# A fifth pair of column blocks by seven products, with the convolution two blocks earlier and three sums of h on GpSimd beside it

## The reference, cut to what matters

```
h = rms_norm(x)
proj = h @ w_in        # r_q r_k r_v r_g | m_q m_k m_v m_o | m_i m_f | gate_r gate_m
ret = retention(rotary(r_q), rotary(r_k), r_v)       # 4 heads, 4 chunks of 128 tokens, a state from chunk to chunk
ret = head_norm(ret) * silu(r_g);       y_ret = ret @ w_ret_branch
qk = silu(conv4(m_q, m_k) + b)          # 4 taps along the tokens
hm = mlstm(q, k, m_v, m_i, m_f) * sigmoid(m_o)       # 4 heads, 4 chunks, a state from chunk to chunk
y_m = head_norm(hm) @ w_mlstm_branch
x += (sigmoid(gate_r) * y_ret + sigmoid(gate_m) * y_m) @ w_out
x += mixture of 32 experts (two per token);  rms_norm
```

## Time and profile before

| | |
|---|---|
| three runs, us | 1027.02, 1027.93, 1027.90 |
| profiled execution, us | 1028.9 |
| its span, first to last instruction, us | 1027.0 |
| busy PE / DVE / ACT / POOL, share of the span | 98% / 48% / 31% / 11% |
| transfers, MB and mean GB/s | 268.21 and 261 |
| chain that ended last, largest parts | PE 78%, SP's queue 12%, DVE 4% |

### The profile page before, as it was taken

One profiled execution on the slowest core, in us unless ns is written; L12 is line 12 of the kernel. 1 busy time (PEld: TensorE's weight loads), 2 busy tenths in 40 slices (PEclk: granted clock), 3 DMA queues, 4 the chain that ended last, 5 costly groups with the idle time before them and its releaser, 6 DMA issues.

```text
span 1027.0 us, 13106 instructions
## 1 busy us (share of the span) xinstructions
PE 1002.9 (98%) x4941; PEld 650.3 (63%) x4941; DVE 494.0 (48%) x796; ACT 316.9 (31%) x524; POOL 108.9 (11%) x119
## 2 busy tenths in 40 slices
PE   8999999999999999999999999999999999999895
PEld 7888888899988988888885433333333333333333
DVE  6267556567778768645525123233233333332235
ACT  6343564455555656622213000000000000000012
POOL 0688300030000000000000000000000000000000
PEclk9999999999999999999998999999999999999998
DMA  9223221422433525162989799999999999999993
GB/s 329 83 83 126 80 82 42 155 37 81 118 103 105 184 42 182 64 210 85 409 318 358 312 419 421 419 420 420 420 420 421 420 421 420 420 420 422 420 413 142
DMA packets 62579, 268.21 MB, mean 261 GB/s; under 512 B 9456, under 2 KB 9648, under 8 KB 37816
## 3 DMA queue, kind: packets, MB, share of 16 engines
q1 hardware_dynamic: 57464, 257.32, 63.1%
q0 software_dynamic: 4800, 9.98, 4.2%
q10 hardware_dynamic: 256, 0.10, 0.0%
HBM read 267.36 MB, written 4.20 MB: 264 GB/s over the span
## 4 chain that ended last, share of the span: by engine, by line
PE 78%; SPq 12%; DVE 4%; DMA 3%; issue 1%; ACT 1%; DVEq 0%; ACTq 0%
PE pj L648 30%; PE pj L923 14%; PE pj L825 13%; SPq L549 8%; PE pj L949 7%; SPq L546 4%; PE cb L605 3%; DMA raw_moe<-in_w_up_dram 3%; PE cb L959 2%; PE cb L960 2%; DVE sg L1934 1%; PE pj L891 1%; PE cb L668 1%; DVE raw_mix L1617 1%; PE cb L697 1%
## 5 line engine op out<-in xcount | busy, mean ns | idle before, releaser
L923 PE MATMUL pj<-raw_moe,xT 128*64 128x512 f32 x1016 | 227.6, 595 | 4.6 <-DMA raw_moe<-in_w_up_dram 2.5
L1458 DVE TENSOR_TENSOR wl<-raw_mix,wh 128x1024 fp32r<-128x1024 f32 x112 | 145.5, 1301 | 144.7 <-ACT wh L1103 144.4
L1918 DVE TENSOR_TENSOR x<-x,cb 128x512 f32<-128x512 f32 x120 | 77.0, 683 | 190.6 <-PE cb L960 190.6
L923 PEld LDWEIGHTS pj<-raw_moe,xT 128*64 128x64 f32 x1016 | 72.1, 137 | 141.2 <-issue 141.2
L1103 ACT ACTIVATE wh<-raw_mix 128x1024 fp32r<-128x1024 f32 x112 | 118.3, 1059 | 113.4 <-PE pj L648 75.8
L949 PE MATMUL pj<-raw_moe,hf 128*64 128x512 f32 x512 | 116.7, 598 | 1.7 <-ACT hf L1404 1.7
L949 PEld LDWEIGHTS pj<-raw_moe,hf 128*64 128x64 f32 x512 | 35.1, 136 | 66.9 <-issue 66.6
L648 PE MATMUL pj<-wh,hTh 128*128 128x512 f32 x192 | 76.5, 398 | 0.7 <-DVE hTl L1489 0.7
L648 PE MATMUL pj<-wl,hTh 128*128 128x512 f32 x192 | 74.9, 390 | 0.0
L648 PE MATMUL pj<-wh,hTl 128*128 128x512 f32 x192 | 74.8, 390 | 0.0
L1409 ACT ACTIVATE yh<-pj,now 128x512 fp32r<-128x512 f32 x32 | 20.5, 684 | 157.8 <-PE cb L960 143.6
(11 more groups left out here) (387 smaller groups left out, 1757.3 us busy)
## 6 DMA issues: line engine op xcount, KB each, us to landing
raw_moe<-in_w_gate_dram SPq DMA_DIRECT2D x64, 1024.0 KB, 26.5
raw_moe<-in_w_down_dram SPq DMA_DIRECT2D x64, 1024.0 KB, 26.6
raw_moe<-in_w_up_dram SPq DMA_DIRECT2D x63, 1024.0 KB, 26.5
raw_mix<-in_w_in_dram SPq DMA_DIRECT2D x32, 1024.0 KB, 5.6
raw_mix<-in_w_in_dram POOLq DMA_DIRECT2D x8, 512.0 KB, 5.8
raw_mix<-in_w_ret_branch_dram SPq DMA_DIRECT2D x4, 1024.0 KB, 6.5
raw_mix<-in_w_mlstm_branch_dram SPq DMA_DIRECT2D x4, 1024.0 KB, 5.5
raw_mix<-in_w_out_dram SPq DMA_DIRECT2D x4, 1024.0 KB, 5.1
```

Of the source, the lines that this page charges most:

```text
L923: mm = nc.tensor.matmul(pj[a * CAP:(a + 1) * CAP, up, :], xT[:, 4 * half + k, a * CAP:(a + 1) * CAP], weights_of(m + a)[:, k, :], start=ha ...
L1458: V.tensor_tensor(wl[:, q % RING, :, :], entry_source(q), wh[:, q % RING, :, :].bitcast(F32), ALU.subtract).then_inc(wl_ok, 1)
L1918: V.tensor_tensor(part, part, cb[:, 2 + g % 2, :], ALU.add).then_inc(c_add, 1)
```

## The change

- `FAST` gets the pair m_v as its first entry, so that m_v's two plain blocks become seven products; the plain blocks are now six, in the order r_q, r_k, m_q, m_k, r_v (two), and what stood beside blocks 2 and 3 stays beside blocks 2 and 3.
- The convolution moves to blocks 3 and 4. For m_q ScalarE applies Silu in one go, and VectorE's product falls away; for m_k all stays. `convx` gets a second buffer, so the copies of the second block don't wait for the first's convolution.
- The retention runs by pairs of heads: steps 0 to 7 (heads 0 and 1) two to a step of block 5, steps 8 to 15 (heads 2 and 3) one to a half x = 0 to 8 and their outputs up to x = 9.
- The mLSTM moves to x = 17 to 40, its decays to x = 9 to 13, the products of its queries to x = 12, 13, 15 and 20.
- GpSimd waits for the turned q and then forms `first21`, `second` and `fourth`, each term in four pieces of 256 columns; `third` follows when the convolution is over.
- The places of some tiles and the waits of the first quadrants change with it.

```diff
-B_RQ, B_RK, B_RV, B_MQ, B_MK, B_MV, B_RG, B_GR, B_GM, B_MO, B_WR, B_WM, B_WO = 0, 1, 2, 4, 5, 6, 8, 10, 12, 14, 16, 18, 20
+B_RQ, B_RK, B_MQ, B_MK, B_RV, B_MV, B_RG, B_GR, B_GM, B_MO, B_WR, B_WM, B_WO = 0, 1, 2, 3, 4, 6, 8, 10, 12, 14, 16, 18, 20
-FAST = (B_GR, B_RG, B_GM, B_MO)
+FAST = (B_MV, B_GR, B_RG, B_GM, B_MO)
+F0 = B_MV
-GATINGS = (5, 6, 11, 12, 14, 15, 18, 24)
-ATTENTION = [1 + (26 * i + 7) // 15 for i in range(16)]
+GATINGS = (5, 6, 11, 12, 15, 19, 20, 24)
+ATTENTION = [17 + (23 * i + 7) // 15 for i in range(16)]
+ML_FIRST = ATTENTION[0]
+DECAYS = (9, 10, 11, 12)
+DECAY_EXPS = (10, 11, 12, 13)
+QUERIES = (12, 13, 15, 20)
...
-        convx = at("convx", 80, [P, 4, 3 + T])
+        convx = [at(f"convx{s}", k, [P, 4, 3 + T]) for s, k in enumerate((80, 128))]
...
+        def ret_step(n):
+            return n % 8 // 2, 2 * (n // 8) + n % 2
...
                 if p == 0:
-                    sp.wait_ge(r_o, 12)
...
+                    sp.wait_ge(wl_ok, 4 * F0 - 4)
+                    quadrant(p, U_11, 0, 0)
+                    sp.wait_ge(wl_ok, 4 * F0 - 2)
+                    quadrant(p, U_T3, 0, 1)
+                    sp.wait_ge(conv_v, 4)
+                    quadrant(p, U_22, 1, 1)
+                    sp.wait_ge(wl_ok, 4 * F0)
+                    quadrant(p, U_21, 1, 0)
+                    return
+                if p == 1:
+                    sp.wait_ge(r_o, 14)
...
                         x = 2 * (PRODUCTS * p + u) + s
                         product_half(p, u, s)
-                        if x == 0:
+                        if x <= 8:
+                            ret_products(7 + x)
+                        if x <= 7:
+                            ret_scores(8 + x)
+                        if x == ML_FIRST - 1:
                             ml_scores(0)
...
+            def decay_exps(j):
+                if j == 0:
+                    act.wait_ge(gex_in, 1)
+                    nc.scalar.activation(gex[:, :, :], gex[:, :, :], ACT.Exp).then_inc(gex_ok, 1)
+                act.wait_ge(dt_in, j + 1)
+                nc.scalar.activation(dT[:, j, :], dT[:, j, :], ACT.Exp, scale=-1.0).then_inc(dt_ok, 1)
+                for c in range(TT):
+                    m = nc.scalar.activation(gbc[:, j, c * P:(c + 1) * P], gbc[:, j, c * P:(c + 1) * P], ACT.Exp, scale=-1.0,
+                                             bias=gcol[:, 3, 4 * j + c:4 * j + c + 1])
+                m.then_inc(wint_ok, 1)
...
                     if b in (B_MQ + 1, B_MK + 1):
                         n = 4 * (b - B_MQ - 1) + j
                         dst = (mqT, mkT)[n // 4]
                         act.wait_ge(free[j], b)
...
-                        nc.scalar.activation(dst[:, j, :], convx[:, j, 3:3 + T], ACT.Identity, scale=vcol[:, 56 + n:57 + n], bias=vcol[:, 24 + n:25 + n]).then_inc(conv_a, 1)
+                        nc.scalar.activation(dst[:, j, :], convx[n // 4][:, j, 3:3 + T], ACT.Identity, scale=vcol[:, 56 + n:57 + n], bias=vcol[:, 24 + n:25 + n]).then_inc(conv_a, 1)
                         act.wait_ge(conv_v, n + 1)
-                        if n >= 1:
+                        if n < 4:
+                            nc.scalar.activation(dst[:, j, :], dst[:, j, :], ACT.Silu).then_inc(mqk_ok, 1)
+                        else:
                             act.wait_ge(mqk_ok, n)
-                        nc.scalar.activation(csg[:, :], dst[:, j, :], ACT.Sigmoid).then_inc(conv_s, 1)
+                            nc.scalar.activation(csg[:, :], dst[:, j, :], ACT.Sigmoid).then_inc(conv_s, 1)
+                    if b == B_MK:
+                        act.wait_ge(rkT_ps, j + 1)
+                        nc.scalar.activation(rkT[:, :, j * P:(j + 1) * P], cb[:, j, :].rearrange("p (h l) -> p h l", h=H), ACT.Copy).then_inc(rkT_ok, 1)
...
             def combined(dst, first, terms):
                 for n, (term, op) in enumerate(terms):
-                    m = G.tensor_tensor(dst[:, :, :], (dst if n else first)[:, :, :], term.bitcast(F32), op)
+                    for k in range(4):
+                        m = G.tensor_tensor(dst[:, k, :], (dst if n else first)[:, k, :], term[:, k, :].bitcast(F32), op)
...
+            pool.wait_ge(rqT_ok, TT)
             combined(first21f, hTh[:, low, upper].bitcast(F32),
                      ((hTh[:, high, upper], ALU.subtract), (hTl[:, low, upper], ALU.add), (hTl[:, high, upper], ALU.subtract)))
             pool.wait_ge(rope_ok, 2 * TT + 1)
             combined(secondf, first21f, ((hTh[:, low, lower], ALU.subtract), (hTl[:, low, lower], ALU.subtract)))
-            pool.wait_ge(rqT_ok, TT)
+            pool.wait_ge(rope_ok, 2 * TT + 2)
+            combined(fourthf, secondf, ((hTh[:, high, lower], ALU.add), (hTl[:, high, lower], ALU.add)))
+            pool.wait_ge(mqk_ok, 8)
+            pool.memset(mva[:, :, :, DV:DA], 1.0)
             combined(thirdf, hTh[:, low, lower].bitcast(F32),
                      ((hTh[:, low, upper], ALU.subtract), (hTl[:, low, lower], ALU.add), (hTl[:, low, upper], ALU.subtract)))
-            pool.wait_ge(rope_ok, 2 * TT + 2)
-            pool.wait_ge(r_s, 16)
-            combined(fourthf, secondf, ((hTh[:, high, lower], ALU.add), (hTl[:, high, lower], ALU.add)))
```

More of the change, by code:

```diff
@@ L510, in _ @@
             sp.dma_start(bif[:, 1:2], b_f.rearrange("l h -> h l")).then_inc(wg_in, 16)
-            for n in range(MIX_RAW, 2 * B_RG):
+            for n in range(MIX_RAW, 2 * F0):
                 mix_chunk(n)
@@ L830, in product_half @@
                         m.then_inc(pair_used, 1)
-            for b in range(1, B_RG):
+            for b in range(1, F0):
                 block_of(b)
@@ L1323, in fast_half @@
                 after = ATTENTION.index(x - 1) if x - 1 in ATTENTION else -1
-                i = 0 if x == 1 else after + 1
-                if (x == 1 or after >= 0) and i < 12:
+                if x <= 9:
+                    ret_output(6 + x)
+                i = 0 if x == ML_FIRST else after + 1
+                if (x == ML_FIRST or after >= 0) and i < 12:
                     act.wait_ge(m_s, i + 1)
@@ L1350, in _ @@
             turned = {2 * (PRODUCTS * w[0] + w[1]) + w[2]: n[0] for w, n in TURNS.items() if len(w) == 3}
-            for b in range(B_RG):
+            for b in range(F0):
                 evict_block(b - 1)
                 block_of(b)
-            evict_block(B_RG - 1)
-            ret_output(15)
+            evict_block(F0 - 1)
             for p in range(len(FAST)):
@@ L1745, in block_of, with decays, queries @@
                         ml_normed(1 - (b - B_WR), b - B_WR)
-                if b == B_RV:
+                if b == B_MQ:
                     rq_turned(3)
+            def decays(j):
+                if j == 0:
+                    dve.wait_ge(gb_in, 16)
+                for c in range(TT):
+                    m = V.scalar_tensor_tensor(dT[:, j, c * P:(c + 1) * P], gbc[:, j, c * P:(c + 1) * P], gcol[:, 0, 4 * c + j:4 * c + j + 1],
+                                               kc[:, K_NOTYET:K_NOTYET + P], ALU.subtract, ALU.add)
+                m.then_inc(dt_in, 1)
+            def queries(j):
+                if j == 0:
+                    dve.wait_ge(mqk_ok, 8)
+                dve.wait_ge(wint_ok, j + 1)
+                V.tensor_tensor(gbc[:, j, :], gbc[:, j, :], mqT[:, j, :], ALU.mult).then_inc(wq_ok, 1)
             def upper_left(p, s):
-                dve.wait_ge(free[s], B_RG + 4 * p + U_11 + 1)
+                dve.wait_ge(free[s], F0 + 4 * p + U_11 + 1)
                 dve.wait_ge(full[2 + s], full_fast(p, U_21, s))
@@ L1756, in upper_right @@
             def upper_right(p, s):
[L1758 removed]
+                dve.wait_ge(free[s], F0 + 4 * p + 2)
                 h = home(p, 0, 1, s)
@@ L1824, in _ @@
             dve.wait_ge(c_in, 48)
-            for b in range(B_RG):
+            for b in range(F0):
                 block_of(b)
-            dve.wait_ge(r_out, 16)
-            dve.wait_ge(gex_ok, 1)
             for p in range(len(FAST)):
```

278 lines of the change are left out of this document (136 added, 142 removed).

## The result

| | before | after |
| --- | --- | --- |
| median of 19 runs each, us | 1027.22 (1025.79 to 1028.3) | 1029.4 (1028.41 to 1032.27) |
| profiled execution, its span, us | 1028.9, 1027.0 | 1029.35, 1027.5 |
| first matmul behind the fast pairs (block `B_WR`), us | 402.44 | 405.94 |
| first matmul of the logits, us | 542.41 | 545.90 |
| first expert's first matmul, us | 566.63 | 567.66 |

The changed kernel is slower by a ratio of 1.0021 (interval 1.0014 to 1.0028), +2.2 us; forecast was 1030.6, and 1029.4 lies within the forecast's own range. The mixer ends 3.5 us later, of which 1.0 us is left at the first expert in the profiled executions (that of the kernel before is one of its longer ones, 1028.9 against a median of 1027.22). So two things need reasons: the +3.5, and where a part of it went.

The account below looks back on a forecast made before the run. Up to 538 us TensorE's columns bound the kernel, then the experts' weight stream. -5.4 + 5.5 + 1.6 + 0.4 + 0.6 = +2.7 us gives 1030.6 us by the median; own range 1028.4 to 1032.5, range of the chances 1023.4 to 1033.2.

Parts of the forecast that it names:

- Products, -5.4: m_v's two plain blocks become seven products, 168 matmuls instead of 192 on TensorE: -5.4 us.
- Stall, +5.5: TensorE waits 5.5 us before block 4 for block 3's first bank, whose copy stands behind ScalarE's last convolution step.
- Turn of 1.14 us: Block 3: VectorE and GpSimd take turns on SBUF, a turn and answer taking 1.14 us, against 0.77 for a tap alone.
- rival of whole pieces: Block 3: each instruction waits for a whole GpSimd piece, step 8.3 us, stall 9.9, total 1034.6 us; chance 0.13.
- Clock, +1.6: After the stall before block 4 TensorE's granted clock may fall: +1.6 us, the middle of bounds 0 and 3.2.
- GpSimd is done early: Block 3's last two steps free of GpSimd's pieces: stall 2.3 us, clock unmoved; 1026.2 to 1027.8 us, chance 0.16.
- Block 4's end, +0.4: After block 4's convolution TensorE waits 0.8 us for a bank's copy or not at all; half counted, +0.4 us.
- x = 15, +0.6: ScalarE, behind with exponentials at x = 9 to 13, evicts x = 13 late, so x = 15 waits for its bank: +0.6 us.
- Retention, 0: The retention's sixteen steps keep the same matmuls and VectorE's work fits between: 0 us, 3 us at most.
- A microsecond of the mixer is one at the end: The experts' weight stream follows the mixer's progress, so each microsecond TensorE wins or loses there counts fully at the end.
- hidden: Blocks 3 and 4: taking turns costs nearly nothing, stalls are 0.3 and 0.8 us, total 1023.6 us; chance 0.23.

Follow-up runs that it names:

- e9: e1 with GpSimd's sums in pieces of 128 columns and VectorE's first masked retention score ahead of a split's tail in block 5: 1021.02 us, ratio 0.9937.
- e2: Changed kernel with GpSimd's three sums beside the convolution left out, a memset in their place: 1023.72 us, ratio 0.997.
- e1: Changed kernel with ScalarE's copies of the m_k and first r_v banks moved between the last convolution step's bias and its Silu: 1022.5 us, ratio 0.9959.
- e3: Changed kernel with each of GpSimd's seven additions as one instruction of 1024 columns, not four of 256: 1031.91 us, ratio 1.0045.
- e6: Changed kernel with GpSimd's sums in pieces of 128 columns in place of 256: 1026.06 us, ratio 0.9992.
- e4: Changed kernel with 22 matmuls that nobody reads on TensorE right ahead of its wait at block 4: 1027.02 us, ratio 1.0001.
- e7: e1 with block 4's copies ahead of the last split and bias, three of four decay steps one half later, two idle matmuls in the routing: 1026.58 us.
- e10: e9 with two idle matmuls in the routing and the decay steps at half-products 9, 9, 12 and 13: 1021.17 us, ratio 0.994.
- e11: e1 with two idle matmuls in the routing and the decay steps at half-products 9, 9, 12 and 13: 1023.11 us, ratio 0.9956.
- e8: e7 with GpSimd's sums in pieces of 128 columns: 1025.09 us, ratio 0.9978.

## Why the prediction was right, step by step

- **Products, -5.4.** Borne out, and a little more: with the waits of blocks 3 to 5 gone (e9) the logits start at 537.14, 5.3 us ahead of before. In that are still 0.65 us of the decays' wait and 0.13 us by which block 3 starts later (85.39 against 85.26), and one wait of before, 0.33 us at 333.02, that e9 doesn't have. The products by themselves gave 5.27 + 0.65 + 0.13 - 0.33 = 5.7 us; where the other 0.3 us come from is not shown.
- **Stall, +5.5.** Measured 5.3, at the place and by the releaser named; splits 7.3 us apart for 7.2, the end of the sums at 117.98 for 118. e2 shows that the sums cause it, e1 that it needs the copies behind the chain.
- **Turn of 1.14 us.** Measured 1.17 (3.52 / 3). e3 and e6 show what a turn is: 0.90, 1.17 and 2.84 us at pieces of 128, 256 and 1024 columns, which take 0.49 (7.81 / 16), 0.71 (2.84 / 4) and 2.40 us in block 5, where `third` meets few taps. A turn is the piece and some 0.4 us, at each size. So the rival of whole pieces was nearer to the mechanism, and wrong in its price: it added the wait for a piece to the full 0.77 of the tap. "SBUF — State Buffer" of the Trainium skill, "SBUF: two separate sides", has the lock for a whole instruction. By that a turn would, as an estimate from these rows, be the piece and the tap, 0.71 + 0.77 = 1.48 us; the trace has 1.17.
- **Clock, +1.6.** The term that was mis-sized: 2.5 by the matmuls' times, 2.6 by e4. The middle of two bounds was taken where the routing's row pointed to the upper one, 3.2; the measured 2.5 lies between. The rival "GpSimd is done early" took a stall of 2.3 us as too short to move the clock; in e6 it fell behind a wait of 2.0 us. "TensorE: Matmul & The Clock Gate" of the Trainium skill, Part 1, says that activity is what releases the throttle. These rows agree: the clock fell in a wait of 5.3 us without a matmul, and stayed at 1.00 where e4 filled it.
- **Block 4's end, +0.4.** Measured 0.5. In block 4 the splits stand 5.44 us apart and not 5.1, since ScalarE there waits for TensorE; the step by itself is 5.1, as e1 shows (121.73 to 126.85).
- **x = 15, +0.6.** The size came out, 0.65 us, by luck: another engine makes the wait at another place. VectorE's subtraction out of a bank, behind a decay step, holds TensorE three halves (x = 12) earlier than named. ScalarE is behind there too, and no wait comes of it. e7, e10 and e11 moved the decay steps and did not remove the 0.65 us, so that the decay step is the cause is not shown either. TensorE's timeline in the changed kernel:

```profile
218.28 0.50 PE L854 MATMUL pj<-wh,hTh 128*128 128x512 f32 x1 [0.65 <-DVE mva L1811]
```

- **Retention, 0.** Held: no wait beside it until e7's copies delayed its first score.
- **A microsecond of the mixer is one at the end.** This held where the routing keeps its clock, and failed for the medians, by a term that the sum didn't have. Against e5, the kernel before with the routing's gaps filled, the changed kernel's logits are 3.4 us later and its span is 3.1 us longer (1027.5 and 1024.4), and e9's logits are 5.35 us earlier and its span 5.3 us shorter. With -5.4 the terms as measured give -5.4 + 5.3 + 2.5 + 0.5 + 0.65 = +3.6, and the logits come 3.5 us later than before. (With the -5.7 and -0.33 above it would be +2.9. Most of the 0.6 us between is that a wait costs 0.16 us more by starts than its bracket says: the row of a matmul lasts 0.39 us, and the next can start after 0.23.) The medians differ by 2.2. The kernel before loses up to 2.5 us in the routing to the low clock, by the spread of its times in a part of its executions; the changed kernel's profile doesn't. e5 shows that filling TensorE's gaps there takes the longer executions of before away. Why the shifted mixer spares the changed kernel that fall stays open; e2's mixer is shifted too, and its profile has lost some clock there (0.93 over 22.91 us).

The forecast change was +2.7 and the measured one +2.2 (the other 0.7 between 1030.6 and 1029.4 is the median of before, 1027.2 over 19 runs and not 1027.9). That it came so near is partly luck, two errors that cancel: the clock taken 0.9 us too small, and 1.3 us that the routing gave back. The lower end of the forecast's own range was also miscounted: 1030.6 - 1.6 - 1.0 is 1028.0 and not 1028.4 (1029.4 lies above both), and the rival "hidden", 1023.6, stands as 1023.4 in the range of the chances.

## What to carry to other kernels

When an engine's instructions turn into a chain through a second engine, look at what stands in its queue behind the chain: copies of finished banks belong into the chain's own waits, not ahead of its next step (e1 against e7), and at a point where the banks are already full (e8). Where VectorE and GpSimd work on SBUF side by side, the size of GpSimd's piece set, in these runs, what each VectorE tap waits; small pieces shorten the chain and lengthen the sum, so they gave some 3 us with the old order (e6) and took the last waits of these blocks away only with the order mended (e9). Price a stall of TensorE with the slow matmuls behind it: here 5.3 us of stall brought 2.5 us more.

## What was not expected of the hardware

A wide addition on GpSimd costs less than its parts: 1024 columns 2.40 us (e3), four of 256 2.84 (the changed kernel), eight of 128 4.36 (e6), all for the first term of `third`. A VectorE instruction that meets one waits out nearly all of it, 2.84 us for a tap of 0.77.

TensorE's granted clock was at 0.50 behind waits of 5.3 us (the changed kernel), 5.8 us (e3), 3.3 us (e7), 2.7 us (e8) and 2.0 us (e6, block 5), and stayed at 1.00 behind those of 1.5 us (e6, block 4) and 1.6 us (e1). A low clock of the kernel before, in the routing, seems to come and go between executions of the same program: one execution was profiled, but its 19 times spread over 2.5 us, and e5, where the gaps are filled, has none of the longer ones.
